# The Mamba layer's output projection: the first input halves of four tiles together, in four accumulators, their second halves behind

## What is computed

```python
def gated_group_rms_norm(y, z, g):
    u = y.astype(jnp.float32) * jax.nn.silu(z.astype(jnp.float32))
    shp = u.shape
    u = u.reshape(shp[:-1] + (SSM_GROUPS, SSM_D_INNER // SSM_GROUPS))
    u = u * lax.rsqrt(jnp.mean(u * u, axis=-1, keepdims=True) + EPS)
    return u.reshape(shp) * g.astype(jnp.float32)
...
    y = gated_group_rms_norm(y.reshape(b, s, SSM_D_INNER), z, gate_norm_g).astype(x.dtype)
    return x + y @ w_out          # (512 x 2048) @ (2048 x 1024)
```

## Time and profile before

| | us |
|---|---|
| median of 3 runs | 1327.17 (1326.48 to 1327.98) |
| the profiled execution, own time | 1329.2 |
| its span, first to last instruction | 1327.3 |
| TensorE busy | 1254.1 (94%) |
| VectorE busy | 846.9 (64%) |
| ScalarE busy | 598.1 (45%) |
| GpSimd busy | 70.9 (5%) |
| mean granted TensorE clock | 0.972 of full |

### The profile page before, as it was taken

One profiled execution on the slowest core, in us unless ns is written; L12 is line 12 of the kernel. 1 busy time (PEld: TensorE's weight loads), 2 busy tenths in 40 slices (PEclk: granted clock), 3 DMA queues, 4 the chain that ended last, 5 costly groups with the idle time before them and its releaser, 6 DMA issues.

```text
span 1327.3 us, 17556 instructions
## 1 busy us (share of the span) xinstructions
PE 1254.1 (94%) x6213; PEld 1026.9 (77%) x6213; DVE 846.9 (64%) x1196; ACT 598.1 (45%) x909; POOL 70.9 (5%) x58
## 2 busy tenths in 40 slices
PE   7899999999979999999997899867999999999997
PEld 6688888888867887777775689865888888888885
DVE  5978888888844356666667559996655422455222
ACT  6457656676633255555555542444332211222112
POOL 0011111011100000000000000121000000000000
PEclk9999999999989999999999799979999999999998
DMA  5333233332314332222221132111333333333332
GB/s 156 108 99 112 80 112 106 100 111 79 110 33 135 95 91 69 64 79 64 63 75 36 48 95 80 55 58 48 95 88 94 95 95 91 94 94 95 110 95 79
DMA packets 203289, 115.57 MB, mean 87 GB/s; under 512 B 3456, under 2 KB 201216, under 8 KB 202224
## 3 DMA queue, kind: packets, MB, share of 16 engines
q1 hardware_dynamic: 201472, 104.50, 27.5%
q0 software_dynamic: 1776, 10.53, 2.3%
HBM read 112.85 MB, written 2.16 MB: 87 GB/s over the span
## 4 chain that ended last, share of the span: by engine, by line
PE 78%; DVE 12%; ACT 5%; issue 4%; DMA 1%; SPq 0%; DVEq 0%; POOL 0%; ACTq 0%
PE psum L508 70%; DVE arena L1784 2%; DVE arena L1635 2%; ACT w_hi L919 2%; PE psum L693 1%; DVE w_lo L1344 1%; PE psum L586 1%; PE psum L594 1%; PE psum L577 1%; PE psum L517 1%; DMA w_raw<-a_w_in 1%; ACT L1116 1%; ACT arena L1116 1%; DVE stat L1639 1%; DVE arena L1647 1%
## 5 line engine op out<-in xcount | busy, mean ns | idle before, releaser
L919 ACT ACTIVATE w_hi<-w_raw 128x1024 fp32r<-128x1024 f32 x191 | 202.1, 1058 | 513.9 <-PE psum L508 512.5
L508 PE MATMUL psum<-a_hi,w_hi 128*128 128x512 f32 (+1 forms) x1000 | 361.3, 380 | 5.9 <-DVE w_lo L1344 5.9
L508 PE MATMUL psum<-a_lo,w_hi 128*128 128x512 f32 (+1 forms) x1000 | 355.8, 374 | 0.0
L508 PE MATMUL psum<-a_hi,w_lo 128*128 128x512 f32 (+1 forms) x1000 | 353.7, 372 | 0.0
L1344 DVE TENSOR_TENSOR w_lo<-w_raw,w_hi 128x1024 fp32r<-128x1024 f32 x191 | 234.3, 1227 | 158.6 <-ACT w_hi L919 158.2
L508 PE MATMUL psum<-b_hi,w_hi 128*128 128x512 f32 x640 | 257.6, 402 | 10.0 <-DVE b_lo L1523 4.1
L508 PE MATMUL psum<-b_lo,w_hi 128*128 128x512 f32 x640 | 256.1, 400 | 0.0
L508 PE MATMUL psum<-b_hi,w_lo 128*128 128x512 f32 x640 | 254.7, 398 | 0.0
L508 PEld LDWEIGHTS psum<-a_hi,w_hi 128*128 128x128 f32 x1000 | 183.7, 191 | 43.5 <-issue 7.2
L508 PEld LDWEIGHTS psum<-a_hi,w_lo 128*128 128x128 f32 x1000 | 183.0, 191 | 33.6
L508 PEld LDWEIGHTS psum<-a_lo,w_hi 128*128 128x128 f32 x1000 | 182.9, 191 | 31.9
(11 more groups left out here) (264 smaller groups left out, 1254.5 us busy)
## 6 DMA issues: line engine op xcount, KB each, us to landing
w_raw<-a_w_in SPq DMA_DIRECT2D x49, 512.0 KB, 3.8
w_raw<-w_up SPq DMA_DIRECT2D x32, 512.0 KB, 3.9
w_raw<-w_down SPq DMA_DIRECT2D x32, 512.0 KB, 3.7
arena<-acs POOLq DMA_DIRECT2D x8, 1024.0 KB, 5.0
w_raw<-a_w_out SPq DMA_DIRECT2D x16, 512.0 KB, 3.7
w_raw<-w_kv SPq DMA_DIRECT2D x16, 512.0 KB, 3.8
w_raw<-b_w_in SPq DMA_DIRECT2D x16, 512.0 KB, 3.8
w_raw<-w_in SPq DMA_DIRECT2D x14, 512.0 KB, 3.6
```

What stands on the lines that cost most here:

```text
L508: ins = mm(out, wv[:, u.par, k, :], xv[:, k0 + k, c0:c0 + cn], start=(first and begin and i == 0 and n == 0), stop=(last and end and i == ...
L919: ac(w_hi[:, u.par, :, :], w_raw[:, u.par, :, :], ACT.Copy).then_inc(S["hi_ready"], 1)
```

## The change

Tiles 0 to 3 are taken together. Units are renumbered: 0 to 3 are the first halves of tiles 0 to 3, 4 to 7 their second halves, with banks 1, 0, 2, 3 as accumulators. The order on TensorE after `ssd_y` becomes: unit 2 whole, 12 matmuls of unit 3, `group_sums`, the other 12, `group_spread`, 18 matmuls of unit 4 (groups 4 to 6), the wait for the last group's operands, its 6 matmuls, units 5 to 7. The loop keeps tiles 4 to 7 in two rounds. SyncE's loads, ScalarE's `hi` and VectorE's `lo` follow the same order; `hi` and `lo` of units 4 and 5 move in between the steps of the last group.

```diff
--- before.py
+++ after.py
@@ -361,10 +361,13 @@
             with sp.Fori(0, 3) as i:
                 group(Lin(2, 2, i))
                 group(Lin(3, 2, i))
-            with sp.Fori(0, 4) as i:
+            for k in range(2):
+                for m in range(4):
+                    load(Lin(U_WOUT + 4 * k + m), t["a_w_out"], k * KT, Lin(m * P))
+            with sp.Fori(0, 2) as i:
                 for k in range(2):
                     for m in range(2):
-                        load(Lin(U_WOUT + 2 * k + m, 4, i), t["a_w_out"], k * KT, Lin(m, 2, i) * P)
+                        load(Lin(U_WOUT + 8 + 2 * k + m, 4, i), t["a_w_out"], k * KT, Lin(4 + m, 2, i) * P)
 
             def head(n):
                 load(n * 4 + U_ATT, t["w_kv"], 0, n * P)
@@ -646,23 +649,39 @@
                 sums(bank(b), v, TOKENS1, S["nst_ready"])
 
 
-            s, m = Lin(GROUPS - 1), Lin(0)
+            def wout_first(j, k, ks=range(KT)):
+
+                u = Lin(U_WOUT + 4 * k + j)
+                pe.wait_ge(S["lo_ready"], (u + 1).v)
+                for n in ks:
+                    for i, (wv, xv) in enumerate(((w_hi, b_hi), (w_hi, b_lo), (w_lo, b_hi))):
+                        ins = mm(bank((1, 0, 2, 3)[j]), wv[:, u.par, n, :], xv[:, k * KT + n, 0:SEQ],
+                                 start=(k == 0 and n == 0 and i == 0), stop=(k == 1 and n == KT - 1 and i == 2),
+                                 skip_group_check=True)
+                if ks[-1] == KT - 1:
+                    ins.then_inc(S["unit_done"], 1)
+
+            s = Lin(GROUPS - 1)
             ssd_turn(s)
             pe.wait_ge(S["ul_ready"], GROUPS // 2)
-            wout(0, m, 0)
+            pe.wait_ge(S["acc_read"], M_WOUT)
+            wout_first(0, 0)
             ssd_states(s)
-            wout(1, m, 0)
+            wout_first(1, 0)
             ssd_y(s)
+            wout_first(2, 0)
+            wout_first(3, 0, range(4))
+            group_sums(s)
+            wout_first(3, 0, range(4, KT))
+            group_spread(s)
             pe.wait_ge(S["ul_ready"], GROUPS - 1)
-            wout(2, m, 1, range(6))
-            group_sums(s)
-            wout(3, m, 1, range(6))
-            group_spread(s)
+            wout_first(0, 1, range(6))
             pe.wait_ge(S["ul_ready"], GROUPS)
-            wout(2, m, 1, range(6, KT))
-            wout(3, m, 1, range(6, KT))
-            with pe.Fori(0, 3) as i:
-                m = Lin(2, 2, i)
+            wout_first(0, 1, range(6, KT))
+            for j in range(1, 4):
+                wout_first(j, 1)
+            with pe.Fori(0, 2) as i:
+                m = Lin(4, 2, i)
                 wout(0, m, 0)
                 wout(1, m, 0)
                 wout(2, m, 1)
@@ -1075,12 +1094,15 @@
             token_decays(s)
             hi(Lin(U_WOUT + 3))
             output_squares(s)
+            hi(Lin(U_WOUT + 4))
             group_root(s)
+            hi(Lin(U_WOUT + 5))
             output_high(s)
-            wout_tile(Lin(0), 0)
-            wout_tile(Lin(0), 1)
-            with act.Fori(0, 3) as i:
-                m = Lin(2, 2, i)
+            for j in range(4):
+                hi(Lin(U_WOUT + 6 + j))
+                wout_tile(Lin(j), 0, False)
+            with act.Fori(0, 2) as i:
+                m = Lin(4, 2, i)
                 hi(m * 2 + (U_WOUT + 2))
                 hi(m * 2 + (U_WOUT + 3))
                 wout_tile(m, 0)
@@ -1565,9 +1587,11 @@
             states(s)
             lo(Lin(U_WOUT + 3))
             output(s)
+            lo(Lin(U_WOUT + 4))
             norm(s)
             normed(s)
             output_low(s)
+            lo(Lin(U_WOUT + 5))
 
 
             def add_squares(m, n, base):
@@ -1575,29 +1599,28 @@
                 if m.reg is None and m.c == 0:
                     return
                 dve.wait_ge(S["sq_ready"], (m + (base + 1)).v)
-                if m.reg is not None:
+                if m.reg is not None or m.c > 1:
                     dve.wait_ge(S["ss_ready"], (m + (2 * (base - base // KT) - 1)).v)
                 tt(ssq[:, 0:n], ssq[:, 0:n], sq[:, m.par, 0:n], ALU.add).then_inc(S["ss_ready"], 1)
 
-            def wout_tile(m, j):
-                u = m * 2 + (U_WOUT + 2 + j)
+            def wout_tile(m, u, out):
+
                 dve.wait_ge(S["unit_done"], (u + 1).v)
-                m = m + j
-                tt(row(h, m, META, T2), row(h, m, META, T2), acc(m + M_WOUT), ALU.add).then_inc(S["acc_read"], 1)
+                tt(row(h, m, META, T2), row(h, m, META, T2), out, ALU.add).then_inc(S["acc_read"], 1)
                 lo(u + 2)
                 add_squares(m, SEQ, 0)
                 dve.wait_ge(S["ah_ready"], (m + 1).v)
                 stt(row(a_lo, m, 0, SEQ), row(h, m, META, T2), par[:, ds((m + C_KVN).v, 1)],
                     f32(row(a_hi, m, 0, SEQ)), ALU.mult, ALU.subtract).then_inc(S["al_ready"], 1)
 
-            wout_tile(Lin(0), 0)
-            wout_tile(Lin(0), 1)
-            with dve.Fori(0, 3) as i:
-                m = Lin(2, 2, i)
+            for j in range(4):
+                wout_tile(Lin(j), Lin(U_WOUT + 4 + j), bank((1, 0, 2, 3)[j]))
+            with dve.Fori(0, 2) as i:
+                m = Lin(4, 2, i)
                 lo(m * 2 + (U_WOUT + 2))
                 lo(m * 2 + (U_WOUT + 3))
-                wout_tile(m, 0)
-                wout_tile(m, 1)
+                for j in range(2):
+                    wout_tile(m + j, m * 2 + (U_WOUT + 2 + j), acc(m + (M_WOUT + j)))
 
             def b_operand(ks):
                 for k in ks:
```

## The result

The changed kernel took 1312.54 us (median of 4 runs, 1310.26 to 1315.70), the kernel before in the same comparison 1326.83 (4 runs, 1325.66 to 1327.98): ratio 0.9894, 95% interval 0.9869 to 0.9919, so a gain of 14.3 us with an interval from 10.7 to 17.4. The forecast was 12.5. Two further comparisons of the same two kernels gave 0.9912 (0.9889 to 0.9934) and 0.9907 (0.9881 to 0.9932). Over all 16 runs of the changed kernel and the 52 runs of the kernel before in these and the experiments' comparisons, the means are 1313.16 and 1325.66: 12.50 us apart, with a standard error of about 0.7 (spreads of single runs 2.2 and 2.7 us). 17 of the 52 come from a comparison in which the changed kernel itself did not run; the three comparisons that timed both give, by their means, 14.1, 13.0 and 12.0 us.

A forecast was written before the change was run, and what follows sets the result against it. TensorE bounds the kernel, busy 94% of the span; 12.7 us were lost to gaps and slow clock at the projection's start. Covering the gaps should gain 12.5: 1327.17 - 12.5 = 1314.7 us, range 1312.7 to 1318.5.

The forecast's parts named there:

- the bound: Stretch from `ssd_y` to the loop: 12.7 of its 25.22 us are lost, the most this order can give back.
- the 0.1 of waiting: TensorE ahead of the last group's operands: a wait of 0.1 us stays of 4.13.
- The slacks: Spare time ahead of `group_sums` (1.15 us), of `output_high` (0.6) and of unit 5's `w_lo` (0.35).
- The addition: GpSimd's sum ahead of `group_sums`: 1.27 us, at worst 0.43 later beside unit 4's `w_lo`, still in time.
- the mild end of the bound: Where GpSimd's addition meets `w_lo`: the addition at most 1.70 us instead of 1.27; nothing charged.
- Unit 5's `w_lo`: VectorE behind `output_low`: ready 0.35 us before TensorE needs it; GpSimd's transfers might cost 0.5 us, taken as 0.
- Lands within 4.7 us: Unit 7's weight load, issued at 394.5 beside GpSimd's transfers, lands at 399.2 and is copied from 400.4.
- the two falls of the clock cost 5.4, 2.7 each: Slow clock behind the gaps around the last group: 5.4 of the 12.7 us lost, the gaps 7.33.
- the allowance of 2 us: Total time: 2 us either way for slow clock stretches further down shifting against the work.
- B: Cover short somewhere around the last group: 3 to 5 us of the loss stay, 1317.7 to 1319.7; chance 0.11.
- C: Four accumulators in turn bring TensorE down to 1.2 GHz: slower, up to 1348 us; chance 0.03.
- D: Gain given back after the projection, in a wait for a transfer: 1325 to 1327 us; chance 0.04.

The follow-up runs named there:

- sums18: Changed kernel with `group_sums` back behind 18 matmuls, as before the change: stretch from `ssd_y` to attention 85.73 us, ratio 0.9953 to the kernel before.
- spread_late: Changed kernel with `group_spread` behind unit 4's 18 matmuls, nothing between it and the last group's operands: stretch 85.25 us, ratio 0.9947 to the kernel before.
- three_acc: Changed kernel with three accumulators: tiles 0 to 2 together, tile 3 by itself behind them; stretch 82.25 us, ratio 0.9917 to the kernel before.
- pool_late: Changed kernel with GpSimd's four transfers held back to the end of unit 8: stretch 79.55 us, ratio 0.9895 to the kernel before.
- fill_before: Kernel before plus unread matmuls, 12 ahead of `group_sums` and 18 behind `group_spread`: stretch 88.20 us against 92.07, ratio 0.9986.
- sums24: Changed kernel with `group_sums` behind 24 matmuls (unit 2), unit 3 whole behind it: stretch 81.26 us, ratio 0.9912 to the kernel before.
- again: The changed kernel once more, nothing altered: stretch 79.55 us, ratio 0.9912 to the kernel before.
- again_b: The changed kernel profiled a third time with more rounds, nothing altered: stretch 79.55 us, ratio 0.9907 to the kernel before.

## Why the prediction was right

**The loss was read rightly.** 12.7 us was the bound, 12.56 came back. In the prediction's steps, counted from the first matmul behind `ssd_y`: `group_sums` at 8.41, measured 8.44; `group_spread` at 12.07, measured 12.12; the operands at 16.80, measured 16.85, with the 0.1 of waiting that was forecast; the attention at 79.5, measured 79.51. sums18 and spread_late show that each move is needed by itself, and three_acc that three accumulators with these weight buffers do not give the whole.

**The slacks held.** The addition took 1.30 and `w_lo` 1.35 beside it, at the mild end of the bound. Unit 5's `w_lo` had 0.42 us to spare, 0.35 by the forecast, and GpSimd's transfers did not slow it.

**Two terms were mis-sized, neither of them one that the 12.5 hangs on.** "Lands within 4.7 us" was 7.0: the row that I took it from was of loads issued some 5 and 7 us behind the first of GpSimd's transfers, while the new order issues one 0.8 us behind. It cost nothing (pool_late). And "the two falls of the clock cost 5.4, 2.7 each", from which the allowance of 2 us was taken, was what the idle times left over, split in half; fill_before, sums18 and spread_late measured 4.6 in all, about 3.1 and 1.4 to 1.5, the larger one behind the shorter gap. Most of the other 0.8 is the tails of the matmuls ahead of the gaps.

**The rivals.** B did not come; sums24 shows how it would have looked, a gap of 1.47 us at a price of 1.75, and that a fall of the clock, as in sums18, is what makes a short cover dear. C did not come: six units in four banks in turn, 376.19 to 411.22 us, and the loop's two banks behind them, all at a clock of 1.00. The Trainium skill (TensorE: Matmul & The Clock Gate, "A second HAM failure mode: psum-queue depth-cycling") tells its rule of one bf16 kernel in which TensorE pauses between the groups of matmuls. Here the change of banks brought no such pause (80.00 of 80 us busy, matmuls 0.23 us apart), so its condition was not met: the prediction's "by that rule this rival would be the outcome" took the rule too widely. D did not come: the first attention matmul stood at 455.70 and the end at 1313.8.

**The total was 1.8 us larger than forecast in the first comparison**, with a median 0.2 us below the range given. No term of the sum shows it: the stretch gave 12.56. By the table it is within the scatter of the two untouched parts, which I had put at 2 us for all of them and which is 6 and 4 us between profiles. The three runs of the kernel before spanned 1.5 us and had hidden that. That the next two comparisons gave less (13.0 and 12.0 by their means) shows how much of a single comparison is chance; the stretch is the surer test.

## What to carry to other kernels

Where a chain of small dependent steps ends a stage, count the independent matmuls that can stand behind each link and move accumulators until each link is covered; what limits this is not the number of banks alone but how many half-done units the weight buffers can hold. Cover first those gaps behind which the trace shows a fall of the clock, down to where it no longer falls: here the first 6 matmuls brought 4.5 us, the next 12 brought 1.75. Read the price of each fall from the trace and not from the length of the gap: 3.1 us behind 2.86, 1.4 behind 4.13. And measure such a change between two instructions of the trace: that figure repeated within 0.04 to 0.2 us, where the interval of a comparison of runs is some 5 to 7 us wide.

## What the runs showed of the hardware that I had not expected

A weight load of 512 KB that is issued 0.8 us behind the first of GpSimd's four transfers takes 7.0 us to land (6.9 in again, 6.7 in again_b) instead of 3.8. And the same 376 us of program, with the same instructions, took from 373.3 to 379.5 us in 13 profiles. In the one trace with 379.5, the clock was at 0.50 for 6.8 us from 14 on and for 6.8 from 65 on; in the one with 373.3 for 3.4 us in all, so most of the 6 us between the two goes with the clock.
